# Padding the slots of a weight ring: where tiles begin modulo 512 bytes in SBUF

## The chip, the cores and the metric

The kernel runs on one core of a Trainium2 chip. The metric is the device time of one execution in microseconds (us). TensorE (PE) multiplies, VectorE (DVE) and ScalarE (ACT) work on tiles in SBUF and PSUM, GpSimd (POOL) only issues some transfers, and SyncE (SP) issues the weight transfers. PE's loading of weights has a row of its own, PEld.

## The reference, cut to what matters

Three transformer-like blocks, one after the other, on 256 tokens of 2048 features, in float32. What matters here is that nearly all the arithmetic is a product of a 256-token activation with a large weight matrix, and that every weight is used once.

```
x = first_block(x, ...)    # latent attention + two-way linear recurrence, gates, w_out
x = second_block(x, ...)   # conv / pool / Fourier mixing, then a gated FFN of 5632
x = third_block(x, ...)    # stick-breaking + sparse attention, then a gated FFN of 5504
...
proj = h @ w_in                                              # first block
hid = silu(x @ w_gate) * (x @ w_up); ffn = hid @ w_down      # second
u = h2 @ w_up; ...; (silu(gate) * val) @ w_down              # third
```

## The kernel before, in words

All weights lie in device memory as 511 slots of 1 MB, in the order of use: 128 partitions of 2048 float32 (`SLOT`), that is four chunks of 128 input features by 512 output features. SyncE carries them one by one into a **ring of four slots** (`ring`, line 222): slot n goes to place n % 4 and its transfer is issued (line 393) as soon as slot n - 4 has been used up (`w_used`).

Most slots (those in `SPLIT`, 477 of them) are multiplied in three float32r products that together give nearly float32 precision. For each half of a slot, 1024 columns:

- ACT copies the half from the ring, rounded to float32r, into a **high part** (line 1158; lines 1171 and 1183 in the recurrence and in the attention of the first block). The high parts have a ring of their own with four half slots: `HI_1` up to the gates of the first block, `HI_Z2` (two half slots) inside its attention, and `HI` from `br_rwkv` on, which is the later three quarters of the execution (`high_ring`, line 377).
- DVE subtracts the high part from the ring's half and writes the difference, the low part, back over that half (line 1837, and 1845 in the same places). `ring_parts` is the same memory as `ring` under the type float32r.
- PE then goes over the half in tiles of 128 input by 128 output features (`by_parts`, line 436 on). Per tile it does three products into the same PSUM place, each with a weight load of 128 columns of its own and 256 moved columns: high weights with the high part of the activation (line 462), high weights with its low part (463), low weights with its high part (464). Lines 641 to 643 and 588 to 590 are the same triple in the gates and in the attention of the first block. At lines 480 to 482 the roles are turned: the activation is loaded, and 512 columns of weights are moved.

ACT may write a half slot of high parts when PE has used the one two slots earlier (`half_used`, `w_used`); DVE waits for ACT (`hi_ready`), PE for DVE (`lo_ready`). All loops are in program order on each engine; the order is written out by hand.

The places in SBUF are fixed in the program. The ring is allocated first after some constants, at byte 1152 of each partition; then come constants, parameters, residual, and at the end the working region `W`, padded to begin at a multiple of 512 bytes (`work_at`), in which every other tile has a hand-written offset in words. Activations lie at multiples of 1024 bytes of `W` there (`H`, `X_HI`, `X_LO`, `HID_HI` and so on), except in the third block, where `HS_HI` begins at 256 and `O3_LO` at 128 modulo 512.

```
ring = sb("ring", [P, RING, SLOT])                          # 222: four slots of 8192 bytes
HI = own("ring_hi", 35504, 4, SLOT // 2)                    # 344: four half slots of 4096 bytes
...
A(high_ring(n)[:, 2 * (e % 2) + half, :], ring[...half...], ACT.Copy)              # 1158
tt(lo, x, high_ring(n)[:, e % 4, :].bitcast(F32), ALU.subtract)                     # 1837
mm(o, w_hi[:, k, cols], hi(kc), ...)                                                # 462
mm(o, w_hi[:, k, cols], lo(kc), ...)                                                # 463
ins = mm(o, w_lo[:, 2 * half + k, cols], hi(kc), ...)                               # 464
```

Of the kernel before, what the change touches and what calls it, by code (L numbers as in the profile page):

```python
# [10 lines left out]
F32R = mybir.dt.float32r  # L11
# [6 lines left out]
P = 128  # L18
# [4 lines left out]
KPS = 4  # L23
SLOT = KPS * COLS
RING = 4
WORK = 39600
HEADS = 8
RANK = 512
NOPE, ROPE = 128, 64
# [38 lines left out]
def slot0(stage, j=0):  # L68

    return FIRST[stage][0] + FIRST[stage][1] * j  # L70
# [134 lines left out]
def build_program(nc, a):  # L205
# [3 lines left out]
    def sb(name, shape, dt=F32):  # L209
        return ctx.enter_context(nc.sbuf_tensor(name, shape, dt))  # L210
# [4 lines left out]
    def S(name):  # L215
        if name not in sems:
            sems[name] = ctx.enter_context(nc.semaphore(name))
        return sems[name]


    ring_at = -(-nc.sbuf_base // 32) * 32
    ring = sb("ring", [P, RING, SLOT])
    ring_parts = nc.alloc_sbuf_tensor_at("ring_parts", [P, RING, SLOT], F32R, offset=ring_at)
    CON = sb("con", [P, N_CONST])
    PR = sb("par", [P, max(NPAR)])
    X = sb("resid", [P, DC, T])
# [9 lines left out]
    assert work_at % 512 == 0  # L236
    W = sb("work", [P, WORK])
    PS = ctx.enter_context(nc.psum_tensor("ps", [P, 8, 512], F32))

    def w(at, *shape):  # L240

        n = int(np.prod(shape))
        v = W[:, at:at + n]
        names = "abcde"[:len(shape)]
        if len(shape) == 1:
            return v
        return v.rearrange(f"p ({' '.join(names)}) -> p {' '.join(names)}", **{k: s for k, s in zip(names[1:], shape[1:])})

    def own(name, at, *shape, dt=F32R):


        return nc.alloc_sbuf_tensor_at(name, [P, *shape], dt, offset=work_at + 4 * at)[:]
# [72 lines left out]
    at += 4096  # L325
    assert at <= WORK, at

# [13 lines left out]
    GU, GU2, GU3 = w(30720, 4, T), w(31744, 4, T), own("gu", 32768, 4, T, dt=F32)  # L341
    P2, P2_HI, P2_LO = w(33792, 2, T), own("p_hi", 34304, 2, T), own("p_lo", 33792, 2, T)
    BROW = w(20736, 2 * COLS)
    HI = own("ring_hi", 35504, 4, SLOT // 2)


    Q_SB, K_SB, V_SB = w(4096, 8, T), w(6144, 8, T), w(8192, 2, WIDTH)
# [29 lines left out]
    def high_ring(n):  # L377

        return HI if n >= slot0("br_rwkv") else HI_1

# [25 lines left out]
    def _(pe):  # L406
# [540 lines left out]
        for s in range(4):  # L947
# [3 lines left out]
            for half in range(2):  # L951
                pe.wait_ge(S("lo_ready"), 2 * e + half + 1)
                w_hi = HI[:, 2 * (e % 2) + half, :].rearrange("p (k a b c) -> p k a b c", k=KPS // 2, a=2, b=2)
                for k in range(KPS // 2):
# [2043 lines left out]
```

How the kernel before makes its waits and increments, by code:

```python
    def wait(self, sem, more=0):  # L160
        self.n[sem.name] = self.n.get(sem.name, 0) + more
        self.eng.wait_ge(sem, self.value(sem))
# [220 lines left out]
    @block.sync  # L384
    def _(sp):
        for k in range(4):
            sp.dma_start(X[:, 4 * k:4 * k + 4, :], a["x"][:, 4 * k:4 * k + 4, :]).then_inc(S(f"x_loaded{k}"), 16)
        for k in range(RING):
            sp.dma_start(ring[:, k, :], a["weights"][k]).then_inc(loaded[k], 16)
        with sp.Fori(0, (SLOTS - RING) // RING) as i:
            for k in range(RING):
                sp.wait_ge(w_used, i * RING + k + 1)
                sp.dma_start(ring[:, k, :],
                             a["weights"][bass.ds(i * RING + RING + k, 1), :, :].rearrange("a p n -> (a p) n"))\
                    .then_inc(loaded[k], 16)
        for n in range(SLOTS - SLOTS % RING, SLOTS):
            sp.wait_ge(w_used, n - RING + 1)
            sp.dma_start(ring[:, n % RING, :], a["weights"][n]).then_inc(loaded[n % RING], 16)
        for k in range(4):
            sp.wait_ge(S("out_ready"), k + 1)
            sp.dma_start(a["out"][:, 4 * k:4 * k + 4, :], OUT[:, 4 * k:4 * k + 4, :]).then_inc(S("out_stored"), 16)
        sp.wait_ge(S("out_stored"), 64)
# [7 lines left out]
        def weights(n, i=None, step=0):  # L410
            v = 16 * (n // RING + 1)
            pe.wait_ge(loaded[n % RING], v if i is None else v + i * (16 * step // RING))
            return ring[:, n % RING, :]
# [595 lines left out]
        def sb_out(q):  # L1010
            pe.wait_ge(S("sb_weights"), q + 1)
            for n in range(4):
```

## Time and profile before

| | |
|---|---|
| device time, median of 2 runs | 3394.03 us (3393.74 to 3394.32) |
| span of the profiled execution, first to last instruction | 3388.4 us |
| PE busy | 3255.3 us (96%), 30322 matmuls |
| PEld busy | 3103.4 us (92%) |
| DVE busy | 2275.4 us (67%) |
| ACT busy | 1517.0 us (45%) |
| POOL busy | 74.3 us (2%) |
| weight transfers | 511 of 1 MB, 4.8 us from issue to landing (median) |
| memory traffic | 654.70 MB read, 6.29 MB written |

The profile gives the span alone for the profiled execution; the 5.6 us between it and the median of the runs lie before the first and behind the last instruction, or are the difference of one run from another. Busy times of different engines overlap. Matmuls are pipelined: a matmul is booked as busy for 0.28 us while the next begins 0.12 us after it, so how fast PE goes is seen from how many matmuls begin in a stretch, not from the busy time of one.

### The profile page before, as it was taken

What the parts mean: (1) busy time and instruction counts of PE and PEld (TensorE: products, weight loads), DVE (VectorE), ACT (ScalarE), POOL (GpSimd) and SP (SyncE); (2) the same over time, 40 slices, a digit from 0 to 9 for tenths busy, and PEclk for the clock granted to TensorE, in tenths of its full rate; (3) what the DMA queues carried; (4) which work ended last, traced back from release to release, by engine and by line L of the source; (5) the groups of instructions that cost most, each with busy time, mean ns of one, the idle gap of its engine ahead of it and who ended that gap; (6) DMA issues with size and microseconds to landing.
All of it is one profiled execution on the core that took longest, in us unless ns stands there. A gap on an engine that the chain in (4) does not pass through costs nothing.

```text
span 3388.4 us, 71888 instructions
## 1 busy us (share of the span) xinstructions
PE 3255.3 (96%) x30322; PEld 3103.4 (92%) x30322; DVE 2275.4 (67%) x2978; ACT 1517.0 (45%) x1835; POOL 74.3 (2%) x154
## 2 busy tenths in 40 slices
PE   8999899999998999999999999999989999999998
PEld 8998888888898769999999999989879899999998
DVE  8776856565687977777655544565656777777545
ACT  5442454443244035544444343453454555545443
POOL 0000100000000000000000000000000000000000
PEclk9999999999999999999999999999999999999999
DMA  8758723232786544677655555534424455555554
GB/s 322 261 204 329 273 86 107 86 108 92 279 346 238 187 161 175 252 290 283 240 190 194 193 195 198 187 127 165 159 100 163 162 191 192 186 187 193 190 197 152
DMA packets 94146, 664.19 MB, mean 196 GB/s; under 512 B 10353, under 2 KB 10993, under 8 KB 15346
## 3 DMA queue, kind: packets, MB, share of 16 engines
q1 hardware_dynamic: 74736, 540.05, 44.4%
q0 software_dynamic: 14400, 104.86, 8.0%
q10 hardware_dynamic: 4802, 16.12, 1.2%
q8 instruction: 178, 2.92, 0.3%
q14 instruction: 30, 0.25, 0.0%
HBM read 654.70 MB, written 6.29 MB: 195 GB/s over the span
## 4 chain that ended last, share of the span: by engine, by line
PE 86%; DVE 9%; ACT 2%; issue 1%; DMA 1%; ACTq 0%; SPq 0%; DVEq 0%
PE ps L463 22%; PE ps L462 22%; PE ps L464 21%; PE ps L434 4%; PE ps L657 4%; PE ps L641 2%; PE ps L493 2%; PE ps L642 2%; PE ps L643 2%; DVE ring_parts L1837 2%; DVE work L1860 1%; DVE work L2113 1%; PE ps L506 1%; DVE ring_parts L1845 1%; PE ps L650 1%
## 5 line engine op out<-in xcount | busy, mean ns | idle before, releaser
L1837 DVE TENSOR_TENSOR ring_parts<-ring,ring_hi 128x1024 fp32r<-128x1024 f32 x866 | 1042.1, 1223 | 701.2 <-ACT ring_hi L1158 687.3
L1158 ACT ACTIVATE ring_hi<-ring 128x1024 fp32r<-128x1024 f32 x866 | 909.4, 1059 | 1141.6 <-PE ps L464 1094.9
L463 PE MATMUL ps<-h_lo,ring_hi 128*128 128x256 f32 x2624 | 729.2, 278 | 0.0
L462 PE MATMUL ps<-h_hi,ring_hi 128*128 128x256 f32 x2112 | 593.1, 281 | 15.8 <-DVE h_lo L1867 8.5
L464 PE MATMUL ps<-h_hi,ring_parts 128*128 128x256 f32 x2112 | 585.1, 277 | 0.0
L463 PEld LDWEIGHTS ps<-h_lo,ring_hi 128*128 128x128 f32 x2624 | 497.7, 190 | 1.4 <-issue 1.2
L462 PE MATMUL ps<-x_hi,ring_hi 128*128 128x256 f32 x1664 | 466.3, 280 | 9.7 <-DVE x_lo L1867 5.8
L463 PE MATMUL ps<-x_lo,ring_hi 128*128 128x256 f32 x1664 | 462.9, 278 | 0.0
L464 PE MATMUL ps<-x_hi,ring_parts 128*128 128x256 f32 x1664 | 461.0, 277 | 0.0
L462 PEld LDWEIGHTS ps<-h_hi,ring_hi 128*128 128x128 f32 x2112 | 397.0, 188 | 18.2 <-issue 9.8
L464 PEld LDWEIGHTS ps<-h_hi,ring_parts 128*128 128x128 f32 x2112 | 397.0, 188 | 0.0
L462 PE MATMUL ps<-hid_hi,ring_hi 128*128 128x256 f32 x1392 | 388.6, 279 | 0.0
L463 PE MATMUL ps<-hid_lo,ring_hi 128*128 128x256 f32 x1392 | 385.6, 277 | 0.0
L464 PE MATMUL ps<-hid_hi,ring_parts 128*128 128x256 f32 x1392 | 384.2, 276 | 0.0
L462 PEld LDWEIGHTS ps<-x_hi,ring_hi 128*128 128x128 f32 x1664 | 313.1, 188 | 10.2 <-issue 6.2
L463 PEld LDWEIGHTS ps<-x_lo,ring_hi 128*128 128x128 f32 x1664 | 316.4, 190 | 0.0
L464 PEld LDWEIGHTS ps<-x_hi,ring_parts 128*128 128x128 f32 x1664 | 313.1, 188 | 0.0
L463 PEld LDWEIGHTS ps<-hid_lo,ring_hi 128*128 128x128 f32 x1392 | 263.1, 189 | 0.0
L462 PEld LDWEIGHTS ps<-hid_hi,ring_hi 128*128 128x128 f32 x1392 | 260.3, 187 | 0.0
L464 PEld LDWEIGHTS ps<-hid_hi,ring_parts 128*128 128x128 f32 x1392 | 260.3, 187 | 0.0
L462 PE MATMUL ps<-hs_hi,ring_hi 128*128 128x256 f32 x768 | 216.6, 282 | 2.7 <-DVE ring_parts L1837 2.7
L464 PE MATMUL ps<-hs_hi,ring_parts 128*128 128x256 f32 x768 | 212.6, 277 | 0.0
(471 smaller groups left out, 5781.3 us busy)
## 6 DMA issues: line engine op xcount, KB each, us to landing
ring<-in_weights SPq DMA_DIRECT2D x511, 1024.0 KB, 4.8
work<-in_ada POOLq DMA_DIRECT2D x96, 1024.0 KB, 6.7
work<-in_c_row POOLq DMA_DIRECT2D x4, 1024.0 KB, 5.6
gate_store<-gate_out ACTq DMA_DIRECT2D x8, 512.0 KB, 6.2
work<-gate_store ACTq DMA_DIRECT2D x2, 2048.0 KB, 19.4
resid<-in_lora ACTq DMA_DIRECT2D x9, 256.0 KB, 5.4
resid<-in_x SPq DMA_DIRECT2D x4, 512.0 KB, 6.0
resid<-in_x ACTq DMA_DIRECT2D x1, 2048.0 KB, 28.0
```

The costliest lines, as they stand in the source:

```text
L434: ins = mm(PS[:, b + m // 2, (m % 2) * T:(m % 2 + 1) * T], ws[:, k, m * P:(m + 1) * P], rhs(kc), start=(kc == 0 and m % 2 == 0), stop=(kc ...
L462: mm(o, w_hi[:, k, cols], hi(kc), start=(kc == 0 and m % 2 == 0), stop=False, skip_group_check=True)
L463: mm(o, w_hi[:, k, cols], lo(kc), start=False, stop=False, skip_group_check=True)
L464: ins = mm(o, w_lo[:, 2 * half + k, cols], hi(kc), start=False, stop=(kc == last - 1), skip_group_check=True)
L493: ins = mm(PS[:, b + m, :], lhs(kc, m), ws[:, k, :], start=(kc == 0 and not biased), stop=(kc == per * KPS - 1), skip_group_check=True)
L506: ins = mm(PS[:, bank, 0:T], ones, src[:, k, :], start=(begin and k == first), stop=(end and k == first + count - 1))
L641: mm(o, w_hi[:, k, cols], h1_hi(kc), start=(kc == 0 and m % 2 == 0), stop=False, skip_group_check=True)
L642: mm(o, w_hi[:, k, cols], h1_lo(kc), start=False, stop=False, skip_group_check=True)
L643: ins = mm(o, w_lo[:, 2 * half + k, cols], h1_hi(kc), start=False, stop=(kc == DC - 1), skip_group_check=True)
L657: return mm(out, lhs, rhs, start=start, stop=stop, skip_group_check=True)
L1158: A(high_ring(n)[:, 2 * (e % 2) + half, :], ring[:, n % RING, half * (SLOT // 2):(half + 1) * (SLOT // 2)], ACT.Copy)\
L1837: tt(lo, x, high_ring(n)[:, e % 4, :].bitcast(F32), ALU.subtract).then_inc(S("lo_ready"), 1)
```

## The change

Each of the four ring slots becomes 2064 words long instead of 2048 (`STAGGER` is 16 words, 64 bytes), and the tile is then cut to its first 2048 words, so the padding is never read or written. The same is done with the four half slots of `HI` (1040 words instead of 1024), which also moves 48 words down; the working region grows by 16 words. `HI_1` and `HI_Z2` are not touched. No instruction is added, taken away or moved.

```
-WORK = 39600
+WORK = 39616
+STAGGER = 16
...
-    ring = sb("ring", [P, RING, SLOT])
-    ring_parts = nc.alloc_sbuf_tensor_at("ring_parts", [P, RING, SLOT], F32R, offset=ring_at)
+    ring = sb("ring", [P, RING, SLOT + STAGGER])[:, :, 0:SLOT]
+    ring_parts = nc.alloc_sbuf_tensor_at("ring_parts", [P, RING, SLOT + STAGGER], F32R, offset=ring_at)[:, :, 0:SLOT]
...
-    HI = own("ring_hi", 35504, 4, SLOT // 2)
+    HI = own("ring_hi", 35456, 4, SLOT // 2 + STAGGER)[:, :, 0:SLOT // 2]
```

By the program's arithmetic, the places modulo 512 bytes are:

| | before | after |
|---|---|---|
| ring slots 0, 1, 2, 3 | 128, 128, 128, 128 | 128, 192, 256, 320 |
| `HI` half slots 0, 1, 2, 3 | 192, 192, 192, 192 | 0, 64, 128, 192 |
| `HI_1`, `HI_Z2` | 192 | 192 |
| activations in `W` | 0 (`HS_HI` 256, `O3_LO` 128) | the same |
| constants, parameters, residual, sums | | 256 bytes further |
| working region `W` | 0 | 0, 512 bytes further |

## Rows read from the trace of the kernel before

**Rows 1.** The page's busy times: engine, us, share of the span, instructions.
```profile
PE 3255.3 (96%) x30322; PEld 3103.4 (92%) x30322; DVE 2275.4 (67%) x2978; ACT 1517.0 (45%) x1835; POOL 74.3 (2%) x154
```

**Rows 2.** The page's chain of work that ended last, by engine and by line.
```profile
PE 86%; DVE 9%; ACT 2%; issue 1%; DMA 1%; ACTq 0%; SPq 0%; DVEq 0%
PE ps L463 22%; PE ps L462 22%; PE ps L464 21%; PE ps L434 4%; PE ps L657 4%; PE ps L641 2%; PE ps L493 2%; PE ps L642 2%; PE ps L643 2%; DVE ring_parts L1837 2%; DVE work L1860 1%; DVE work L2113 1%; PE ps L506 1%; DVE ring_parts L1845 1%; PE ps L650 1%
```

**Rows 3.** Stretches: length, busy us and instructions by engine, granted clock, DMA share, GB/s.
```profile
20.00:285.00 265.00, 259.97 (x2179) 256.83 (x2180) 210.74 (x224) 122.34 (x132) 10.73 (x21) 0.99 0.68 248
285.00:340.00 55.00, 52.78 (x208) 39.06 (x206) 35.64 (x30) 13.22 (x16) 5.32 (x10) 1.00 0.96 399
...
1050.00:1115.00 65.00, 54.99 (x405) 53.38 (x406) 48.29 (x70) 22.07 (x33) 2.65 (x5) 0.92 0.60 223
...
3136.00:3375.00 239.00, 239.00 (x2069) 238.79 (x2067) 122.76 (x115) 99.42 (x103) 0.00 (x0) 1.00 0.51 181
```

**Rows 4.** The same view, stretches in which PE never stops.
```profile
133.50:153.50 20.00, 20.00 (x175) 20.00 (x174) 16.41 (x18) 8.12 (x8) 1.06 (x2) 1.00 0.93 354
157.00:177.00 20.00, 20.00 (x172) 20.00 (x171) 16.20 (x18) 7.70 (x8) 1.07 (x2) 1.00 0.92 347
...
1550.00:1650.00 100.00, 100.00 (x868) 100.00 (x867) 71.76 (x65) 45.36 (x43) 4.79 (x9) 1.00 0.77 285
...
2560.00:2630.00 70.00, 70.00 (x608) 70.00 (x607) 40.60 (x39) 29.26 (x29) 0.00 (x0) 1.00 0.53 192
3200.00:3300.00 100.00, 100.00 (x868) 100.00 (x867) 46.57 (x41) 43.89 (x48) 0.00 (x0) 1.00 0.54 191
```

**Rows 5.** Stretches before and after 895 us, line 462 alone: PE and PEld.
```profile
0.00:895.00 895.00, 199.43 (x704) 132.97 (x704) 0.99 0.52 193
895.00:3388.40 2493.40, 1691.66 (x6032) 1132.91 (x6032) 0.99 0.55 197
```

**Rows 6.** Groups of instructions: the first product of the gates, line 641.
```profile
L641 PE MATMUL ps<-h_hi,ring_hi 128*128 128x256 f32 x512 | 151.8, 296 | 0.0
```

**Rows 7.** Timeline at 2417 us: start us, duration us, what; 512 columns of weights moved.
```profile
2417.04 0.39 PE L480 MATMUL ps<-ring_hi,hs_hi 128*128 128x512 f32 x1
...
2417.27 0.39 PE L481 MATMUL ps<-ring_hi,h_lo 128*128 128x512 f32 x1
...
2417.50 0.39 PE L482 MATMUL ps<-ring_parts,hs_hi 128*128 128x512 f32 x1
...
2417.73 0.39 PE L480 MATMUL ps<-ring_hi,hs_hi 128*128 128x512 f32 x1
```

**Rows 8.** A stretch of line 434 alone, unsplit float32 products of 256 columns.
```profile
300.00:320.00 20.00, 20.00 (x95) 17.58 (x93) 1.00 0.87 356
```

**Rows 9.** Groups of instructions on DVE and ACT, 1024 columns each: count, busy us, mean ns.
```profile
L1837 DVE TENSOR_TENSOR ring_parts<-ring,ring_hi 128x1024 fp32r<-128x1024 f32 x866 | 1042.1, 1223 | 701.2 <-ACT ring_hi L1158 687.3 <-DVE uc L2702 5.4 <-DVE mod L2460 3.0
L1845 DVE TENSOR_TENSOR ring_parts<-ring,ring_hi 128x1024 fp32r<-128x1024 f32 x88 | 106.2, 1215 | 9.2 <-ACT ring_hi L1171 8.8 <-DVE resid L2663 0.2
L2457 DVE TENSOR_TENSOR hid_lo<-gu,hid_hi 128x1024 f32 x11 | 13.5, 1226 | 1.4
L1158 ACT ACTIVATE ring_hi<-ring 128x1024 fp32r<-128x1024 f32 x866 | 909.4, 1059 | 1141.6 <-PE ps L464 1094.9 <-DMA ring<-in_weights 33.3 <-PE ps L968 6.3
```

**Rows 10.** The same view for ACT from 918 to 945 us.
```profile
L1416 ACT ACTIVATE m_hi<-work 128x1024 fp32r<-128x1024 f32 x3 | 3.2, 1065 | 4.4 <-DVE work L2204 4.4
```

**Rows 11.** The waits: who waited for whom, us in total, times, longest.
```profile
ACT ring_hi L1158 <- PE ps L464: 1094.9, 668, 8.4
...
ACT ring_hi L1158 <- DMA ring<-in_weights: 33.3, 4, 24.0
...
PE ps L462 <- DVE ring_parts L1837: 20.4, 13, 3.8
```

**Rows 12.** DMA queues: packets, MB, share of 16 engines' span.
```profile
q1 hardware_dynamic: 74736, 540.05, 44.4%
q0 software_dynamic: 14400, 104.86, 8.0%
```

## The prediction

> **What bounds the kernel now.** I read the page's busy times first, then the chain of waits, then stretches of the execution. PE is busy in 96% of the span [rows 1], and the chain that ended last lies to 86% on PE, most of it in the three products of the split weights, lines 462 to 464 [rows 2]. DVE holds 9% of the chain and ACT 2%. A look by stretches shows where [rows 3]: in the last long stage (3136 to 3375 us) PE is never idle; in the first (20 to 285 us) and in the conv projection (1050 to 1115 us) it waits a few us; only the 55 us from 285 us on have the DMA engines nearly full (0.96).
>
> So the question is how fast PE goes when it never stops, and whether that depends on where tiles begin. Here the busy time says nothing and the count says all [rows 4]. In 100 us there are 868 matmuls; one is booked for 0.28 us while the next begins 0.12 us later, so about two of them began before the window: 866, or **115.5 ns** each. It is the same number from 1550 us on, where DVE works 72% and ACT 45% of the time, and from 3200 us on, where they work 47% and 44%: what the other two stream through SBUF does not show in it.
>
> **The change part by part.** It adds no instruction, wait or transfer. It only moves starting places, so each part is a question of whether some instruction gets longer or shorter.
>
> *PE.* The kernel before holds a few natural experiments. From 2560 to 2630 us the moved operands begin at 256 (`HS_HI`) and 128 (`O3_LO`) modulo 512 and the low weights at 128, so in one product of three the weights being loaded begin at the same place as the operand being moved. Everywhere else the operands are at 0 and the weights at 192 and 128. The count there is 608 - 2 in 70 us, again 115.5 ns [rows 4]. Where the roles are turned, weights at 192 and 128 are moved and activations at 256 and 0 are loaded: three products of 512 columns take 0.69 us [rows 7], 115 ns per 256 columns, though they have half as many weight loads per column. What PE spends over its columns thus goes with the columns moved and not with how a load lies to an operand. From this I cost the change on PE at **0**.
>
> There is one row against it. From 157 to 177 us PE is as little interrupted as from 133.5 to 153.5 us, with the same instructions on tiles at the same places and the same granted clock of 1.00; yet it begins 172 - 2 matmuls in 20 us instead of 175 - 2: **117.6 ns** [rows 4]. So a second, slower pitch exists, 2.1 ns above the first, which a run of matmuls can fall into after a stop. Nothing in these rows ties it to a starting place; but if the two streams of PE can lock to each other in two ways, then starting places that change from half slot to half slot may choose between them. It is the bound for PE: split products are 704 + 6032 triples [rows 5] and 512 in the gates [rows 6], 7248 triples or 21,744 matmuls, and 2.1 ns on each is 46 us. No row of this kind shows a faster pitch; the bound on that side is half of an unsplit product, (95 - 2) in 20 us or 215 ns [rows 8], so 107.5 ns: 8 ns times 21,744 is 174 us. I take zero, because it is the row nearest to what changes: other relative places, same pitch.
>
> The Trainium skill (SBUF — State Buffer, section "Who interferes with whom") says that PE and ACT never wait on anyone, and gives PE two independent read ports, one for the moved operand and one for weight loads. By that rule no placement matters to PE and the time stays at 3394 us. The row at 117.6 ns shows a stall that the rule has no name for, so I don't raise the chance of no change on account of it.
>
> *DVE and ACT.* The subtraction of 1024 columns takes 1223 ns with its inputs at 128 and 192, and 1226 ns on line 2457 where both inputs and the output begin at 0; line 1845 has 1215 ns [rows 9]. The copy on ACT takes 1059 ns from 128 to 192 and 1065 ns from 0 to 0 [rows 9, 10]. After the change the two inputs of a subtraction begin 0 to 256 bytes apart, by slot; 0 and 64 apart are these rows. Lines 1837 and 1845 hold 3% of the chain [rows 2], 102 us, and (1226 - 1215)/1223 of that is 0.9 us either way. ACT's 2%, 68 us, by 6/1059 is 0.4 us. The rest is covered: ACT waits 1094.9 us for PE to release a half slot, and PE in line 462 waits 20.4 us in all for DVE [rows 11]. I take 0. If that cover went, DVE's wait for ACT and then PE's 20.4 us would grow.
>
> *Transfers.* Queue 1, mostly the ring, takes 44.4/540.05 = 0.0822% of the engines per MB, queue 0 takes 8.0/104.86 = 0.0763%, 7% less [rows 12]. If all of that were a matter of places, it would count where DMA is full, 55 us [rows 3]: 3.9 us either way at most. Elsewhere the loads are hidden; ACT waited for them four times, 33.3 us, of which one wait was 24.0 [rows 11]. I take 0, since the places modulo 512 of the ring stay a mix.
>
> *The other tiles.* Constants, parameters and residual move by 256 bytes, the working region by 512. The same rows speak for 0.
>
> **Sum.** 3388.4 us of span + 0, with bounds of 0.9 + 0.4 + 3.9 = 5 us apart from PE's; the median of the runs is 5.6 us over that span, which I add unchanged: **3394 us**.
>
> **The rivals.** *Slower: PE falls into the slower pitch.* Its place is the split products, above all from 895 us on, where the high weights begin at 0 in one half slot of four, together with the moved operand. If all products went at 117.6 ns: 3394 + 46 = 3440 us, still within 2%; if half did, 3417. What a measurement of this kernel can tell from no change is about 2%, 68 us; that needs 3.1 ns per matmul, one and a half of the steps seen. Two steps, 4.2 ns, would give 3394 + 92 = 3486 us. For it speaks that the second pitch exists; against it, that the four other windows of rows 4 all stand at 115.5 to 115.6, the one with other places among them.
>
> *Faster: the 8 ns over 107.5 are a clash of equal starting places, which padding dissolves.* All of it gives 3394 - 174 = 3220 us, a step of 2.1 ns 3348 us. For it speaks only that 115.5 is not 107.5; against it, rows 7: half the loads per column, the same cost per column.
>
> *The change does less than it says.* Up to 895 us the high parts keep their one place, since `HI_1` and `HI_Z2` are not padded: in 704 + 512 of 7248 triples only one load of three moves. The operands stay at 0 throughout. This trims either rival by a tenth and gives 3394 us by itself; it is counted with the forecast.
>
> **How the numbers follow.** No change to within 6 us: 0.76. Slower pitch, up to one step: 0.13, of which half lies below 3420 us; more than 2% slower: 0.04. Faster by less than 2%: 0.04; by more: 0.03. The range 3380 to 3420 holds the forecast, the lesser half of the slower case and a little of the faster one, about 0.84. Within 2%: 0.76 + 0.13 + 0.04 = 0.93.
>
> **What would show it.** In the profile after, the windows that PE never leaves should again hold 868 matmuls in 100 us; lines 1837 and 1158 should stand at 1223 and 1059 ns within 10 ns; ACT should go on waiting for PE. The forecast is wrong if the count in the two long feed-forward stages is 852 (117.6 ns) or less, or 885 and more, or if the pitch goes by slot.

## The result, and the profile after

The kernel after takes **3435.8 us** (median of 2 runs, 3433.74 to 3437.87) against 3394.03 us: a ratio of **1.0121, interval 1.0097 to 1.0146**. The prediction was 3394 us and its range ended at 3420 us: it was wrong, by 42 us. The profiled execution has a span of 3432.4 us, 44.0 us more than before's 3388.4. In the code after, every line named here stands one further down (462 is 463, 1837 is 1838).

The page of the kernel after: busy times, queues, chain, and the groups that answer to [rows 1, 2, 9, 12].

```profile
PE 3301.0 (96%) x30322; PEld 3148.9 (92%) x30322; DVE 2275.3 (66%) x2978; ACT 1517.1 (44%) x1835; POOL 74.3 (2%) x154
...
q1 hardware_dynamic: 74736, 540.05, 43.7%
q0 software_dynamic: 14400, 104.86, 7.9%
...
PE 86%; DVE 9%; ACT 2%; DMA 2%; issue 1%; ACTq 0%; SPq 0%; DVEq 0%
...
L1838 DVE TENSOR_TENSOR ring_parts<-ring,ring_hi 128x1024 fp32r<-128x1024 f32 x866 | 1041.6, 1223 | 728.9 <-ACT ring_hi L1159 715.4
L1159 ACT ACTIVATE ring_hi<-ring 128x1024 fp32r<-128x1024 f32 x866 | 909.4, 1059 | 1177.8 <-PE ps L465 1122.7
```

The whole difference is on one engine. PE is busy 45.7 us longer with the same 30322 products. DVE has 2275.3 us against 2275.4 and ACT 1517.1 against 1517.0. The subtraction still takes 1223 ns and the copy 1059 ns [rows 9], to the nanosecond, although three of four slots and of four half slots have moved. The queues' shares are lower only because the span is longer: 43.7% of 3432.4 us is 1500 us, 44.4% of 3388.4 was 1504.

The waits of the kernel after, as in [rows 11]: who waited for whom, us in total, times, longest.

```profile
ACT ring_hi L1159 <- PE ps L465: 1122.7, 667, 8.4
...
ACT ring_hi L1159 <- DMA ring<-in_weights: 42.2, 8, 23.9
...
PE ps L463 <- DVE ring_parts L1838: 22.3, 12, 6.5
```

ACT waits 28 us more for PE to release a half slot (1122.7 against 1094.9); PE waits 2 us more for DVE. The other engines wait longer for PE, and PE hardly longer for them: PE got slower by itself.

The stretches that answer to [rows 3, 4], kernel after (length, then busy us and count by engine, granted clock, DMA share, GB/s).

```profile
20.00:285.00 265.00, 261.04 (x2179) 257.90 (x2180) 210.22 (x223) 121.82 (x130) 10.11 (x20) 0.99 0.68 248
...
1550.00:1650.00 100.00, 100.00 (x854) 100.00 (x853) 72.20 (x67) 46.45 (x43) 4.78 (x9) 1.00 0.75 280
2700.00:2800.00 100.00, 100.00 (x853) 100.00 (x852) 73.10 (x103) 50.04 (x48) 0.00 (x0) 1.00 0.51 183
3200.00:3300.00 100.00, 100.00 (x854) 100.00 (x853) 46.76 (x42) 40.63 (x41) 0.00 (x0) 1.00 0.55 193
```

In the first stage the count did not change: 2179 matmuls in 265 us, as before. In the long stages 853 or 854 stand where 868 stood, at the same granted clock of 1.00, the 2.4 GHz level. Less the two that began earlier, 853 is 851 in 100 us: 117.5 ns instead of 115.5, 2.0 ns more per matmul. Adding up in the trace the distance from each product of line 462 (463) to the start of the third one after it gives, from 895 us on, 2128.7 us before and 2170.6 after: 41.9 of the 44.0 us. Before 895 us line 462 gives 0.7 us more (254.2 and 254.9) and the gates 0.3 (195.5 and 195.8).

Below, three products of one tile (the lines 462, 463 and 464 of before) are a **triple**; its time runs from start to start. Before takes 346.7 ns per triple, 3 x 115.5. The kernel after has a different time in each half slot. The timeline of the kernel after from 1510 us on (start us, duration us, what), cut to the first product of each half slot of eight triples.

```profile
1510.45 0.28 PE L463 MATMUL ps<-x_hi,ring_hi 128*128 128x256 f32 x1
...
1513.17 0.28 PE L463 MATMUL ps<-x_hi,ring_hi 128*128 128x256 f32 x1
...
1516.04 0.29 PE L463 MATMUL ps<-x_hi,ring_hi 128*128 128x256 f32 x1
...
1518.88 0.28 PE L463 MATMUL ps<-x_hi,ring_hi 128*128 128x256 f32 x1
...
1521.68 0.28 PE L463 MATMUL ps<-x_hi,ring_hi 128*128 128x256 f32 x1
...
1524.51 0.28 PE L463 MATMUL ps<-x_hi,ring_hi 128*128 128x256 f32 x1
...
1527.38 0.28 PE L463 MATMUL ps<-x_hi,ring_hi 128*128 128x256 f32 x1
...
1530.21 0.28 PE L463 MATMUL ps<-x_hi,ring_hi 128*128 128x256 f32 x1
...
1533.03 0.28 PE L463 MATMUL ps<-x_hi,ring_hi 128*128 128x256 f32 x1
...
1535.75 0.28 PE L463 MATMUL ps<-x_hi,ring_hi 128*128 128x256 f32 x1
```

Eight triples take 2.72 us (340 ns each), then 2.87 (359), 2.84, 2.80, 2.83, 2.87, 2.83, 2.82, and with the next turn of the ring 2.72 again. In the stretch from 1490 to 1540 us the times of the single triples repeat to the nanosecond from one turn to the next. That is no accident of arrival: the time goes with the places of the half slot. I write a pair as low weights/high weights, each the place of its tile in bytes modulo 256 counted from the moved operand, which begins at 0; 256 and 320 modulo 512 are 0 and 64 then. The means over the feed-forward stages, without the triples that a stop lengthened beyond 400 ns: 128/0 358.0, 128/64 354.9, 192/128 350.6, 192/192 353.1, 0/0 358.7, 0/64 353.6, 64/128 353.4, 64/192 340.6. Their mean is 352.9; 6.2 ns more than 346.7, times 6032 triples [rows 5], is 37 us. Before's own pair, 128/192, still stands at 346.6 in the output projections of the kernel after, where it occurs among others. The first stage has such differences too, since the low weights move there: 344.3 ns with them at 64, 353.4 to 353.6 at 192 and 0, and 350.0 on the mean against 347.4 before. PE stops more often there, and its stops were 1.1 us shorter in all, so that little of it is seen in the sum.

### The profile page after: what moved, and what is told of

The parts are those of the page before. It is cut to its first block, busy times and chain, and to the rows that moved or that the text cites. A ratio compares the mean times of both kernels' runs of the same rounds, so it can differ in the third digit from the quotient of the medians.

```text
span 3432.4 us, 71888 instructions
## 1 busy us (share of the span) xinstructions
PE 3301.0 (96%) x30322; PEld 3148.9 (92%) x30322; DVE 2275.3 (66%) x2978; ACT 1517.1 (44%) x1835; POOL 74.3 (2%) x154
## 3 DMA queue, kind: packets, MB, share of 16 engines
q1 hardware_dynamic: 74736, 540.05, 43.7%
## 4 chain that ended last, share of the span: by engine, by line
PE 86%; DVE 9%; ACT 2%; DMA 2%; issue 1%; ACTq 0%; SPq 0%; DVEq 0%
PE ps L463 21%; PE ps L465 21%; PE ps L464 21%; PE ps L658 4%; PE ps L435 4%; PE ps L642 2%; PE ps L494 2%; PE ps L643 2%; PE ps L644 2%; DVE work L1861 2%; DVE ring_parts L1838 2%; DMA work<-in_ada 1%; DVE work L2114 1%; PE ps L507 1%; PE ps L651 1%
## 5 line engine op out<-in xcount | busy, mean ns | idle before, releaser
L1838 DVE TENSOR_TENSOR ring_parts<-ring,ring_hi 128x1024 fp32r<-128x1024 f32 x866 | 1041.6, 1223 | 728.9 <-ACT ring_hi L1159 715.4
L1159 ACT ACTIVATE ring_hi<-ring 128x1024 fp32r<-128x1024 f32 x866 | 909.4, 1059 | 1177.8 <-PE ps L465 1122.7
L464 PE MATMUL ps<-h_lo,ring_hi 128*128 128x256 f32 x2624 | 736.7, 281 | 0.0
L465 PE MATMUL ps<-h_hi,ring_parts 128*128 128x256 f32 x2112 | 592.9, 281 | 0.0
L465 PE MATMUL ps<-x_hi,ring_parts 128*128 128x256 f32 x1664 | 468.1, 281 | 0.0
```

Source lines behind the costliest of these rows:

```text
L464: mm(o, w_hi[:, k, cols], lo(kc), start=False, stop=False, skip_group_check=True)
L465: ins = mm(o, w_lo[:, 2 * half + k, cols], hi(kc), start=False, stop=(kc == last - 1), skip_group_check=True)
L1159: A(high_ring(n)[:, 2 * (e % 2) + half, :], ring[:, n % RING, half * (SLOT // 2):(half + 1) * (SLOT // 2)], ACT.Copy)\
```

## The experiments

The theories: **A**, the pair of places sets PE's pitch. **B**, that neighbouring half slots lie at unequal places is what costs, whatever the places. **C**, another tile that was moved along does it. All kernels are the kernel before, edited as shown; of their stretches in which PE never stops one or two of each long stage are shown.

**The ring moved as a whole, no padding** (all pairs 64/192, the fastest pair above):

```diff
-    ring_at = -(-nc.sbuf_base // 32) * 32
+    sb("before_ring", [P, 48]); ring_at = -(-nc.sbuf_base // 32) * 32
```

> All four ring slots at 320 modulo 512, unpadded, all high parts at 192 as before: one pair of places throughout. Theory A (the pitch of the split products hangs on the pair of places of low and high weights, modulo 256, and nothing else): the pair 320/192 had 340 to 341 ns per triple in the changed kernel's trace, so 882 matmuls in 100 us and 3394 - 47 = 3347 us. Theory B (it is the change of place from one half slot to the next that costs): no change of place, so 866 matmuls and 3394 us. Theory C (the other tiles, moved by 256 and 512 bytes, cost it): they are moved here too, 3436 us.

3408.7 us (3391.3 to 3438.8, 10 runs), ratio 1.0056 (1.0016 to 1.0095): neither figure. Its stretches tell why:

```profile
1450.00:1550.00 100.00, 100.00 (x885) 100.00 (x884) 72.77 (x66) 47.13 (x44) 4.76 (x9) 1.00 0.77 288
...
2700.00:2800.00 100.00, 100.00 (x844) 100.00 (x843) 73.29 (x96) 47.98 (x46) 0.00 (x0) 1.00 0.51 184
3200.00:3300.00 100.00, 100.00 (x843) 100.00 (x842) 46.88 (x44) 43.17 (x47) 0.00 (x0) 1.00 0.52 190
```

885 in the second feed-forward stage (883 in 100 us, 113.3 ns, 340 per triple), 844 and 843 in the third (118.9 ns, 356.7 per triple), with the same instructions at the same places. So one pair has **two pitches**, and from 2660 us to its end the third stage never leaves the one that it began with. A in its simple form falls. B falls too: by it, places that never change would have left 3394 us and 866 matmuls everywhere.

**Everything at 0**: ring and all high parts begin where the moved operands begin.

```diff
+    sb("before_ring", [P, 96]); ring_at = -(-nc.sbuf_base // 32) * 32
...
-    HI_1, H1_HI = own("ring_hi1", 18480, 4, SLOT // 2), own("h1_hi", 14336, DC, T)
+    HI_1, H1_HI = own("ring_hi1", 18432, 4, SLOT // 2), own("h1_hi", 14336, DC, T)
...
-    HI = own("ring_hi", 35504, 4, SLOT // 2)
+    HI = own("ring_hi", 35456, 4, SLOT // 2)
```

(`HI_Z2` likewise, from 27184 to 27136.)

> All ring slots and all high parts at 0 modulo 512, where the moved operands are. Theory A: the pair 0/0 had 358.7 ns per triple against 346.7 before, times 7376 triples is 89 us: 3483 us, 836 matmuls in 100 us. Theory B: 3394 us. Theory C: 3436 us.

3479.1 us (3476.2 to 3480.3), ratio 1.0242 (1.022 to 1.0265): A's number within 4 us. No place differs from another here, yet this is the slowest of the uniform kernels, 83 us above before's runs beside it (3396.0). Its stretches:

```profile
1450.00:1550.00 100.00, 100.00 (x836) 100.00 (x835) 69.33 (x64) 45.93 (x43) 4.76 (x9) 1.00 0.72 273
...
2705.00:2710.00 5.00, 5.00 (x25) 5.00 (x25) 5.00 (x13) 4.58 (x12) 0.00 (x0) 0.50 0.00 2
2710.00:2715.00 5.00, 5.00 (x42) 5.00 (x41) 5.00 (x14) 5.00 (x13) 0.00 (x0) 0.94 0.18 26
```

(836 - 2) in 100 us is 119.9 ns, 360 per triple. B, in which uneven places are the cause, is gone. (The last two rows, behind a pause, are for the end of this text.)

**The tiles behind the ring moved by 256 bytes, the ring left alone:**

```diff
-    CON = sb("con", [P, N_CONST])
+    sb("after_ring", [P, 64]); CON = sb("con", [P, N_CONST])
```

> Ring and high parts as before (128 and 192), 256 unused bytes behind the ring, so that constants, residual and working region lie as after the change. Theory A: 3394 us. Theory B: 3394 us. Theory C: 3436 us.

3394.1 us, ratio 0.9981 (0.9959 to 1.0003): C falls. Two of its stretches:

```profile
1450.00:1550.00 100.00, 100.00 (x868) 100.00 (x867) 73.94 (x68) 46.47 (x43) 4.76 (x9) 1.00 0.76 284
2560.00:2630.00 70.00, 70.00 (x597) 70.00 (x596) 39.52 (x39) 30.30 (x30) 0.00 (x0) 1.00 0.51 181
```

The first has 868, as before. The second is the third output projection (`w_out3`), the stretch from which the prediction took its zero [rows 4]: 597 where the kernel before has 608, that is 117.6 ns instead of 115.5, although weights and operands lie to each other as before. By its trace it began at 347 ns per triple and went over to 353 at 2561 us, without a stop. So that row, too, is one of two pitches that its places can have.

**Each half of the change alone.** Only the high parts padded, then only the ring:

```diff
-    HI = own("ring_hi", 35504, 4, SLOT // 2)
+    HI = own("ring_hi", 35456, 4, SLOT // 2 + 16)[:, :, 0:SLOT // 2]
```

(`WORK` grows by 16 words, as in the change.)

> The padding of the later ring of high parts alone; weight ring at 128 as before. Theory A: the four pairs with 128 had 358.0, 354.9, 355.9 and 346.6 ns per triple, mean 353.9, 7.2 above before; 6064 triples from 895 us on: 43 us, so 3437 us. Theory B: places change every half slot, about as much as in the changed kernel: 3430 us. Theory C: the rest is not moved, 3394 us.

```diff
-    ring = sb("ring", [P, RING, SLOT])
-    ring_parts = nc.alloc_sbuf_tensor_at("ring_parts", [P, RING, SLOT], F32R, offset=ring_at)
+    ring = sb("ring", [P, RING, SLOT + 16])[:, :, 0:SLOT]
+    ring_parts = nc.alloc_sbuf_tensor_at("ring_parts", [P, RING, SLOT + 16], F32R, offset=ring_at)[:, :, 0:SLOT]
```

> The padding of the weight ring alone; all high parts at 192 as before. Theory A (the pitch hangs on the pair of places): the four pairs with 192 had 346.7, 353.1, 353.3 and 340.3 ns per triple, mean 348.4, 1.7 above before, times 7376 triples: 12 us, 3406 us. Theory B (every change of place costs): a change after every slot instead of every half, about half of the change's 42 us, 3415 us. With the high parts' 39 us measured alone, parts that add up would leave 3 us, 3397 us.

High parts alone: 3433.4 us, ratio 1.0107 (1.0084 to 1.0129), nearly the whole effect. Ring alone: 3419.5 us, ratio 1.0063 (1.0038 to 1.0089). The two together are not the sum: 37 + 19 us against 42. (The 39 us in the second expectation are against 3394 us; against before's runs beside it they are 37.) The stretches of the kernel with only the ring padded:

```profile
1450.00:1550.00 100.00, 100.00 (x863) 100.00 (x863) 73.28 (x68) 46.45 (x43) 4.78 (x9) 1.00 0.76 282
...
2700.00:2800.00 100.00, 100.00 (x849) 100.00 (x848) 70.79 (x96) 50.40 (x48) 0.00 (x0) 1.00 0.53 188
3200.00:3300.00 100.00, 100.00 (x849) 100.00 (x848) 47.65 (x45) 43.04 (x46) 0.00 (x0) 1.00 0.54 192
```

863 in the second feed-forward stage is what A's pairs give (348 ns per triple on the mean: 128/192 and 64/192 at 347 to 350 and at 340, the other two at 353). In the third all pairs stand at 353 or above, 849. A's 3406 us missed the second pitch there.

**Is it the place against the moved operand, or the place itself?** The moved operands and the working region go 64 bytes up, the weights stay at 128 and 192. Against the operand they are then at 64/128. A fourth theory, **D**, that PE meets the streams of ACT and DVE, was tried with it: the streams of these two over the rings stay where they were, and so do the transfers into the ring.

```diff
-    pad = -(-(-nc.sbuf_base // 32) * 32) % 512 // 4
+    pad = -(-(-nc.sbuf_base // 32) * 32) % 512 // 4 + 16
...
-    HI = own("ring_hi", 35504, 4, SLOT // 2)
+    HI = own("ring_hi", 35488, 4, SLOT // 2)
```

(`HI_1` and `HI_Z2` likewise by 16 words back.)

> Weights where they were (128 and 192), the working region and with it every moved operand 64 bytes further. Theory A-relative (places count relative to the moved operand): the pair is 64/128 seen from the operand, which had 353.5 ns per triple: 3394 + 50 = 3444 us, 849 matmuls in 100 us. Theory A-absolute (places of the weights count by themselves or against each other): 346.7 ns, 3394 us. Rival D (it is ACT's and DVE's reads and writes of the weights that clash with PE): weights don't move, 3394 us.

3450.8 us (3444.1 to 3459.6), ratio 1.014 (1.0116 to 1.0165). No weight moved, and PE is slower: the places of the weights by themselves, or against each other, do not explain the pitch; the operand's place is part of it. Its stretches:

```profile
1270.00:1340.00 70.00, 70.00 (x595) 70.00 (x596) 50.68 (x64) 42.03 (x58) 1.07 (x2) 1.00 0.59 214
1450.00:1550.00 100.00, 100.00 (x836) 100.00 (x835) 70.16 (x64) 44.13 (x41) 4.78 (x9) 1.00 0.72 268
...
3200.00:3300.00 100.00, 100.00 (x845) 100.00 (x844) 54.01 (x56) 42.45 (x44) 0.00 (x0) 1.00 0.53 190
```

The pair 64/128, at 353 in the kernel after, stands at the same 353 in the second output projection (`w_out2`, the row from 1270 us on), which is what A gives when places are counted from the operand; but it runs at 360 and at 356 in the two long stages: again more than one pitch for one pair. Against D also speaks the kernel after: the triple at a given place of a half slot, of a given pair, takes the same time to 1 ns on the mean whether ACT or DVE works beside it or not, wherever both cases occur four times or more.

**Steps of 32 bytes** in place of 64, on both rings (ring at 32, 64, 96, 128; high parts at 160, 192, 224, 0). It asks whether only the 64-byte line counts:

```diff
+    sb("before_ring", [P, 40]); ring_at = -(-nc.sbuf_base // 32) * 32
+    ring = sb("ring", [P, RING, SLOT + 8])[:, :, 0:SLOT]
...
+    HI = own("ring_hi", 35496, 4, SLOT // 2 + 8)[:, :, 0:SLOT // 2]
```

> Padding of 32 bytes: ring slots at 32, 64, 96, 128 and high parts at 160, 192, 224, 256 modulo 256; a map of pairs half a step apart. If a place counts by the 64-byte line it lies in: 354, 353, 340, 354, 354, 340, 347 and 358 ns per triple by half slot, mean 350, so 3394 + 20 = 3414 us. If the distance counts to the byte: pairs between two neighbours lie between their pitches.

One execution, 3442.4 us: not 3414. The pair 64/224 takes 354.8 ns per triple where 64/192 took 340, and 128/0 takes 356.9; 96/192 lies with 346.4 at 128/192. So 32 bytes seem to matter, and the rule by lines does not give these times; since a pair can have more than one pitch, one execution is no proof. A finer rule was not found.

**Two pairs by themselves**, to settle whether a pair fixes the pitch (A1) or only which pitches are possible (A2). All at 192/192, then all at 64/64:

```diff
+    sb("before_ring", [P, 16]); ring_at = -(-nc.sbuf_base // 32) * 32
```

> One pair throughout, 192/192, by moving the ring 64 bytes. The pair had 353.1 to 353.4 ns per triple in the changed kernel and in the ring padded alone, but 340.0 in the kernel with alternating places. Theory A1 (one pitch per pair): 353.2 ns, 3394 + 48 = 3442 us. Theory A2 (a pair has more than one pitch, and a stretch keeps the one it entered at its last stop): stretches at 340 and at 353 side by side, between 3347 and 3442 us, runs apart by tens of us as with 320/192.

```diff
+    sb("before_ring", [P, 48]); ring_at = -(-nc.sbuf_base // 32) * 32
...
-    HI = own("ring_hi", 35504, 4, SLOT // 2)
+    HI = own("ring_hi", 35472, 4, SLOT // 2)
```

(`HI_1` and `HI_Z2` likewise by 32 words back.)

> One pair throughout, 64/64 (ring at 320 modulo 512). The pair had 353.6 ns per triple in the changed kernel and 340 to 341 in the kernel with alternating places. Theory A1: 3394 + 50 = 3444 us. Theory A2: a mix of stretches at 340 and 353, between 3347 and 3444 us.

192/192: 3430.7 us, ratio 1.0096 (1.0071 to 1.012). 64/64: 3392.3 us (3381.5 to 3403.3), ratio 0.9984 (0.9968 to 1.0). First the stretches of 192/192, then those of 64/64:

```profile
1450.00:1550.00 100.00, 100.00 (x851) 100.00 (x850) 70.90 (x64) 44.09 (x41) 4.38 (x9) 1.00 0.76 282
...
3200.00:3300.00 100.00, 100.00 (x851) 100.00 (x850) 47.11 (x44) 40.61 (x42) 0.00 (x0) 1.00 0.54 192
```

The other kernel, 64/64:

```profile
1450.00:1550.00 100.00, 100.00 (x885) 100.00 (x884) 74.93 (x70) 46.58 (x44) 4.77 (x9) 1.00 0.78 290
...
2662.00:2722.00 60.00, 60.00 (x531) 60.00 (x531) 43.20 (x56) 30.96 (x29) 0.00 (x0) 1.00 0.55 193
2742.00:2802.00 60.00, 60.00 (x512) 60.00 (x511) 43.49 (x62) 31.38 (x30) 0.00 (x0) 1.00 0.50 181
...
3200.00:3300.00 100.00, 100.00 (x852) 100.00 (x851) 45.42 (x41) 40.62 (x41) 0.00 (x0) 1.00 0.54 190
```

The third feed-forward stage of 64/64 begins at (531 - 2) in 60 us, 113.4 ns, and goes on at (512 - 2), 117.6 ns, to its end. Between the two lies one hold-up, which its timeline shows (start us, duration us, what):

```profile
2738.11 0.28 PE L463 MATMUL ps<-h_lo,ring_hi 128*128 128x256 f32 x1
2738.22 0.28 PE L464 MATMUL ps<-h_hi,ring_parts 128*128 128x256 f32 x1
2738.40 0.39 PE L462 MATMUL ps<-h_hi,ring_hi 128*128 128x256 f32 x1
2738.63 0.28 PE L463 MATMUL ps<-h_lo,ring_hi 128*128 128x256 f32 x1
```

Two products begin 0.18 and 0.23 us after the one before instead of 0.11: 0.18 us lost in all, and from there on the other pitch, for 600 us. 192/192 stands at 340 ns in one output projection (`w_out`) of the next kernel; here it stands at 353 in that projection and in the long stages, but at 340 for 62 triples between two stops of the first stage (from 134 us on) and for 21 in the conv projection. A2 holds in that a pair has more than one pitch; that runs then lie apart by tens of us came true for 64/64 (22 us) and not for 192/192 (5 us).

**Places that alternate**: ring slots at 192, 64, 192, 64 and half slots of the high parts at 64, 64, 192, 192, so that the feed-forward stages have only the pairs 192/64 and 64/192, the two that stood at 340 in the kernel after.

```diff
+    sb("before_ring", [P, 16]); ring_at = -(-nc.sbuf_base // 32) * 32
+    ring = sb("ring", [P, RING, SLOT + 32])[:, :, 0:SLOT]
...
+    class Apart:
+        def __init__(self, name, at):
+            self.t = [own(f"{name}_{k}", at + 1024 * k + 32 * (k // 2), SLOT // 2) for k in range(4)]
...
+    HI = Apart("ring_hi", 35472)
```

(`HI_1` likewise, from 18448; the working region begins at a multiple of 256 bytes here, not of 512.)

> Ring slots at 192, 64, 192, 64 and high parts at 64, 64, 192, 192 modulo 256, so that in 83% of the slots the pairs low/high are 192/64 and 64/192, which had 340.9 and 340.3 ns per triple in the changed kernel; elsewhere 192/192 and 64/64, 353 ns. Theory A1 (a pair has two pitches, and the change of place at each slot brings PE back to the lower one): 3394 - 6.2 x 6100 ns + 6.6 x 1276 ns = 3365 us. Theory A2 (PE stays in the pitch it fell into at its last stop, as with one pair throughout): between 3365 us and, with 356.7 ns throughout, 3460 us, different from run to run by tens of us. Theory B: 3430 us.

This was written before the two kernels above. Its A1 is that the change of place brings PE back to the lower pitch, its A2 that PE stays in the pitch it fell into.

3359.6 us (3357.8 to 3361.0), ratio **0.9877 (0.9855 to 0.9898)**: faster than before, and 5 us below that A1's 3365. 192/192 and 64/64, which A1 put at 353, stand at 340 in `w_out`; that A2's tens of us from run to run are not seen. In the third output projection its triples still took 353 to 364 ns on the mean of a half slot; there one moved operand, `O3_LO`, begins at 128. So a last kernel adds that tile at 0:

```diff
-    O3, O3_LO = w(31008, DC, T), own("o3_lo", 31008, DC, T)
+    O3, O3_LO = w(31040, DC, T), own("o3_lo", 31040, DC, T)
```

> The kernel with alternating places, and the low part of the attention's output moved by 128 bytes, so that it too begins at 0 modulo 256. The 256 triples of that product had 353 to 364 ns in the kernel with alternating places. Theory A (places count relative to the moved operand): they come to 340 ns like the others, 256 x 18 ns is 4 us less, 3355 us. If the low part's place doesn't count: 3360 us.

3355.8 us (3350.6 to 3359.7), ratio **0.9879 (0.9859 to 0.99)**; that projection's triples now take 340 to 344 ns. The projection first, with `O3_LO` at 128 (70 us from 2540 us on) and at 0 (from 2530 us on), then the page and the stretches of the last kernel:

```profile
2540.00:2610.00 70.00, 70.00 (x589) 70.00 (x589) 38.50 (x37) 28.27 (x28) 0.00 (x0) 1.00 0.51 188
2530.00:2600.00 70.00, 70.00 (x621) 70.00 (x619) 41.50 (x39) 31.14 (x32) 0.00 (x0) 1.00 0.54 191
```

```profile
PE 3213.6 (96%) x30322; PEld 3062.0 (91%) x30322; DVE 2273.5 (68%) x2978; ACT 1517.0 (45%) x1835; POOL 74.1 (2%) x154
```

```profile
1450.00:1550.00 100.00, 100.00 (x885) 100.00 (x884) 74.39 (x67) 46.17 (x43) 4.75 (x9) 1.00 0.77 291
...
2700.00:2800.00 100.00, 100.00 (x882) 99.79 (x881) 72.19 (x98) 52.11 (x49) 0.00 (x0) 1.00 0.56 196
3200.00:3300.00 100.00, 100.00 (x885) 100.00 (x884) 48.63 (x46) 44.97 (x48) 0.00 (x0) 1.00 0.55 200
```

885 in both stages, PE busy 41.7 us less than before [rows 1], ACT as before and DVE within 2 us of it. The two kernels cannot be told apart in their ratios; both beat before and after.

**Half the columns**, to see which of PE's two streams sets the pitch: everything at 0, and in the third feed-forward stage each product moves 128 columns of tokens instead of 256 (the second half of the tokens is left out there).

```diff
+    tk = slice(0, P if slot0("ffn3") <= n < slot0("down3") else T)
+    mm(o[:, tk], w_hi[:, k, cols], hi(kc)[:, tk], start=(kc == 0 and m % 2 == 0), stop=False, skip_group_check=True)
...
```

> All at 0 modulo 512, but in the third block's up projection the products move 128 columns instead of 256 (the second half of the tokens is left out there, and PE's work with it). With 256 columns each product took 120.0 ns. If a weight load of 128 columns is what bounds the pitch, it stays near 110 to 120 ns. If moving bounds it and the loss goes with the columns: 60 ns. If moving bounds it and each load costs a fixed loss over the 113.3 ns of the best pair: 57 + 7 = 64 ns. PE then has stops for DVE, so the pitch is read between them.

One execution, 3873.0 us. The stage became slower, for a reason that I had not expected. Its stretches, at the start of the stage, inside it and behind its end:

```profile
2700.00:2705.00 5.00, 2.13 (x9) 1.38 (x8) 3.68 (x6) 2.68 (x4) 1.82 (x1) 1.00 0.66 210
2705.00:2710.00 5.00, 2.23 (x11) 2.26 (x11) 4.78 (x10) 3.32 (x9) 0.00 (x0) 0.71 0.00 2
2710.00:2715.00 5.00, 5.00 (x25) 5.00 (x25) 5.00 (x15) 5.00 (x13) 0.00 (x0) 0.50 0.00 0
...
2900.00:3600.00 700.00, 700.00 (x3283) 700.00 (x3283) 280.02 (x372) 191.56 (x180) 0.00 (x0) 0.50 0.30 102
...
3610.00:3615.00 5.00, 5.00 (x38) 5.00 (x37) 4.46 (x10) 3.68 (x5) 0.00 (x0) 0.84 0.64 210
3615.00:3620.00 5.00, 5.00 (x45) 5.00 (x43) 4.79 (x7) 2.00 (x2) 0.00 (x0) 1.00 0.53 177
```

3283 products in 700 us are 213 ns each, at a granted clock of 0.50, the 1.2 GHz level. At that level products of 256 columns take as long: in the kernel with everything at 0, 25 in the 5 us from 2705 us on (the row shown with it), and by the start times of the trace 213 ns from one to the next. So half the columns bring nothing; something of which each product has as much as before sets the pitch there. The weight load is one such thing, though no row separates it from the rest. None of the three figures expected can be set against 213 ns, since they were for the 2.4 GHz level: which of PE's streams sets the pitch there stays open.

## Why the prediction was wrong, point by point

- **PE at 0: the step that failed.** I took zero "because it is the row nearest to what changes: other relative places, same pitch". That row [rows 4, the stretch from 2560 us on] was one other pair of places, in one product of three, in one execution, and I read it as independence. The same stretch with the same places stood at 117.6 ns in the kernel with the tiles behind the ring moved: what the row showed was one of two pitches, and by chance the one that most of the kernel had. Its counterpart in the kernel with alternating places shows the opposite: with `O3_LO` at 128 these triples took 353 to 364 ns, with it at 0 they took 340 to 344. The rows of 512 columns [rows 7] bore on it no better: they have one load per 512 columns, and with other places they move too, the other way: in the kernel with everything at 0 three products took 680 ns, less than the 693 of before (medians of 61), where the split products became slower. What PE spends does depend on how a load lies to an operand: 340 to 360 ns per triple.
- **The row against it was the right warning.** The stretch at 117.6 ns [rows 4] showed a second pitch for the same places, and the slower rival priced it: 3440 us if all split products went at it. The kernel after stands at 117.5 ns and 3435.8 us. I gave that rival 0.13 because nothing tied the pitch to a place. That the size came out is in part luck: 117.5 ns is the mean of eight half slots between 340.6 and 358.7 ns per triple, and not one pitch. The pitch goes by half slot, the same in each turn of the ring; that it goes by slot the prediction had named as a sign that it is wrong. As a bound for PE one step of 2.1 ns was too small: with everything at 0 it is 4.4 ns (119.9 against 115.5).
- **The rule that I set beside it.** The Trainium skill (SBUF — State Buffer, "Who interferes with whom") says that PE and ACT never wait on anyone. For ACT the runs agree: its copy took 1059 ns before and after. What I drew from it for PE, that no placement matters and the time stays at 3394 us, they refute: measured are 3356 to 3479 us with the same instructions at other places, and the measurement decides. No run shows PE waiting for another engine over it; what PE waits for inside is open.
- **DVE, ACT, transfers, the other tiles at 0** held: 1223 and 1059 ns; DMA 1500 us of the engines against 1504; 3394.1 us with the tiles behind the ring moved.
- **"The change does less than it says"** held in its place: before 895 us, where `HI_1` and `HI_Z2` stayed, line 462 and the gates together lost 1.0 us. The reason given, that only one load of three moves, does not carry that: the ring alone, which moves that same load, cost 19 us, and in the first stage the triples are 2.6 ns longer.
- **What a measurement can tell** was put at 2%. The interval here reaches 0.25% to either side, so 1.2% is clear of no change.
- **The faster rival** priced a gain of one step, 2.1 ns, at 3348 us. It is there, though not for this padding: 113.3 ns and 3356 us with alternating places.

**What stays open.** Shown is that the pitch changes when the weights are moved and when the moved operand is, that one pair can have several pitches, and that one change from one to the other came with a hold-up of 0.18 us. That the distance from the operand, modulo 256, is all that counts fits the pairs named here and is not shown beyond them. Not shown either is what clashes inside the chip, by what rule in bytes (steps of 32 seem to count), and what chooses the pitch after a hold-up. Nor is it shown why the kernels with alternating places kept 340 ns in the feed-forward stages (their 9 runs lie between 3350.6 and 3361.0 us), when 64/192 alone and 64/64 alone left it in the third.

## What to carry to other kernels

Where PE never stops, read its pitch as matmuls per 100 us, by stage and by buffer slot: a busy share of 100% hides 6%. Treat the start of a weight tile relative to the operand that is moved over it as a tuning parameter, and try several pairs over several runs, since one pair can have two pitches. One place that shows no cost says nothing of the others; a second pitch in the trace of before is a reason to give the change of places a real price.

## What the runs showed of the hardware that was not expected

- The commonest pitches lie 6.67 ns per triple apart: 340, 346.7, 353.3 and 360 ns (885, 868, 851 and 836 matmuls in 100 us), at a granted clock of 1.00. Others lie between, such as the 356 and 356.7 ns above. The kernel before, too, ran at 353.3 in some of its stretches; beside these kernels its runs spread from 3388 to 3418 us.
- **At the 1.2 GHz level the places cost nothing.** Behind a pause PE runs at a granted clock of 0.50 for a few us. By the start times of the trace the products there follow each other after 213 or 214 ns in the kernel before, after, with everything at 0, with the operands at 64 and with alternating places (108 to 147 such products in each), the same for 128 and for 256 columns. Half of 213.3 would be 106.7 ns; at the full level 113.3 to 120 are seen. So what the places decide, up to 6.7 ns per product between these kernels, shows at 2.4 GHz only.
- The granted clock stayed low under unbroken work. In the kernel with 128 columns per product it fell to 0.50 after the pause at 2705 us and stayed there for 900 us in which PE went on without a stop, always with products of 128 columns. From 3609 us on PE had products of 256 columns, and the clock was at 0.84 in the 5 us from 3610 us on and at 1.00 in the next 5. With 256 columns behind the same pause, everything at 0, it was at 0.50 in the 5 us from 2705 us on and at 0.94 in the next 5. Why it stayed low is not shown.
